# Two transformer blocks in split fp32 on one core: the passages between projections in two halves of 256 tokens

## The chip, the cores and the metric

The kernel runs on one core of one Trainium2 chip, as one launch. The metric is the time of one execution in device microseconds (us), as the median of several runs. The engines are PE (TensorE), ACT (ScalarE), DVE (VectorE), POOL (GpSimd) and SP (SyncE); weights arrive by DMA from HBM into SBUF, and matmuls write to PSUM, eight banks of 128 x 512 fp32 values.

## The reference, cut to what matters

512 tokens with 1024 features pass through two blocks. What matters here is the row of projections, and what stands between one and the next:

```python
def rms_norm(x, g):
    xf = x.astype(jnp.float32)
    y = xf * lax.rsqrt(jnp.mean(xf * xf, axis=-1, keepdims=True) + EPS)
    return (y * g.astype(jnp.float32)).astype(x.dtype)

# first_block: modulation, w_in, retention and sparse attention ("mixed"), then
        y = rmsnorm(mixed @ w_out[l], g_post[l])
        x = x + gate[:, None, :].astype(x.dtype) * y
# second_block
        f = swiglu(rms_norm(h, g_ffn1_pre[i]), w_ffn1_gate[i], w_ffn1_up[i], w_ffn1_down[i])
        h = h + 0.5 * rms_norm(f, g_ffn1_post[i])
        u = rms_norm(h, g_mix_pre[i])
        qkv = u @ w_in[i]
...
        h = h + rms_norm(mixed @ w_out[i], g_mix_post[i])
        f = swiglu(rms_norm(h, g_ffn2_pre[i]), w_ffn2_gate[i], w_ffn2_up[i], w_ffn2_down[i])
        h = h + 0.5 * rms_norm(f, g_ffn2_post[i])
        e = (p[i] @ w_ple_proj[i]) * jax.nn.sigmoid(h @ w_ple_gate[i])
        h = h + rms_norm(e, g_ple_post[i])
```

So each output is normed over its 1024 features, scaled, added to the residual, and the sum is normed again before the next projection. The hidden width of the FFNs is 2816, which is 22 tiles of 128.

## The kernel before

Tokens lie along the columns and features on the partitions, so the residual `X` and the input `UH`, `UL` of a projection are 8 tiles of 128 x 512 each. Every matmul of a projection is done in three parts on fp32r operands (`mm3`, L262 to L264): high times high, low times high, high times low. Weights come as a stream of 218 chunks of 512 KB into four slots `RAW`. For each chunk ScalarE makes the high part `WH` (`hi_of_weights`), VectorE subtracts it for the low part `WL` (`lo_of_weights`), two chunks ahead of TensorE, in two slots each.

The phases are, in order, with their chunks: p1 (32, input projection of block one), attention, p2 (8, output projection), f1 (44, gate and up of FFN1), d1 (24, down), p5 (24, input projection of block two), attention, p6 (8, output), f2 (44) and d2 (24) for FFN2, pp (2) and pg (8) for the last gated step. A chunk of p2, f1 and the like is `feature_chunk`: 8 feature tiles in three parts, 24 matmuls of 128x512, into one PSUM bank. In d1 and d2 three chunks make one output of 22 x 3 = 66 matmuls.

Each engine has its own program, written out by hand, and the engines wait for each other by counters: `mm` counts chunks that TensorE has finished, `w_hi` and `w_lo` split chunks, and an `Event` counts one kind of operation.

A *passage* is what stands between two projections. On ScalarE `project_out` and `mlp_down` take the square of each output tile and copy the tile (`Y_H`, `Y_U`); GpSimd adds up the squares (`sum_squares`, L435); TensorE sums over the partitions by two matmuls with ones (`summed_stats`, L1201 and L1203); ScalarE takes the root (`rms`) and VectorE the reciprocal (`rstd`, L814). Then for each of the 8 tiles VectorE forms gain times output times reciprocal (L1040), GpSimd adds it to `X` (L427), ScalarE writes the high part `UH` and the square, VectorE the low part `UL` (L1051 or L1049). The first chunk of the next projection waits tile by tile for `UL`, and the sums of the second norm are 8 matmuls with ones between its tiles (`first_of`, L1196). That norm's reciprocal is applied to the outputs of f1, not to its inputs. While the passage starts, TensorE does 34 matmuls whose result nobody reads (`bridge`, `keep_clock`, L1209):

```python
            def bridge(d):

                pe.wait_ge(w_lo, d + 1)
                keep_clock(34, WH[:, d % 2, 0:SEQ], B[7])
```

At the end the last passage adds to the residual on GpSimd (even tiles) and VectorE (odd tiles, L1029), and SyncE writes the output in 8 DMAs of 256 KB. `X` shares its place with other data during the first attention; GpSimd fetches it anew (L421) before the first passage.

Of the kernel before, what the change touches and what calls it, by code (L numbers as in the profile page):

```python
# [17 lines left out]
P = 128  # L18
SEQ = 512
DM = 1024  # L20
# [33 lines left out]
RAW_SLOTS = 4  # L54
SPLIT_SLOTS = 2
# [5 lines left out]
def build(nc, a):  # L61
    with ExitStack() as ctx:
# [7 lines left out]
        OFF_WL = OFF_WH + 8 * KB  # L70
        OFF_H = OFF_WL + 8 * KB
# [12 lines left out]
        RAW = at("RAW", OFF_RAW, [P, RAW_SLOTS, 1024])  # L84
        WH = at("WH", OFF_WH, [P, SPLIT_SLOTS, 1024], F32R)
        WL = at("WL", OFF_WL, [P, SPLIT_SLOTS, 1024], F32R)

# [45 lines left out]

        EP = hb("EP", 0, [P, KT, SEQ])
# [5 lines left out]
        AL = at("AL", OFF_WL, [P, 4, SEQ], F32R)  # L140
# [48 lines left out]
        raw_here = [sem(f"raw_here{n}") for n in range(RAW_SLOTS)]  # L189
# [19 lines left out]
        class Event:  # L209


            def __init__(self, name):
                self.sem, self.n = sem(name), 0
# [6 lines left out]
        def wait(eng, s, value):  # L220

            if value > 0:
                eng.wait_ge(s.sem if isinstance(s, Event) else s, value)
# [9 lines left out]
        def plan_banks():  # L233
# [10 lines left out]
            for first, up, down, s, n0 in (("p2", "f1", "d1", 1, 0), ("p6", "f2", "d2", 5, FT)):  # L244
# [3 lines left out]
                for m in range(8):  # L248
                    use(first, m, m % 4, E["y_copy"], 8 * ((s - 1) // 2) + m + 1)
# [3 lines left out]
                for m in range(8):  # L253
                    use(down, m, m % 4, E["y_copy"], 8 * ((s + 1) // 2) + m + 1)
            for m in range(8):
                use("pp", m, m % 4, E["ep"], m + 1)
            for m in range(8):
                use("pg", m, m % 4, E["pl_s"], m + 1)

        def mm3(out, lh, ll, rh, rl, start, stop, **kw):  # L260
# [7 lines left out]
            "silu_c converted ada_dot shift x_n gain_cols x_sq y_copy angle sines x_stats x_rms x_rstd u_t u_hi u_lo "  # L268
# [9 lines left out]
        x_odd = Event("x_odd")  # L278
        x_new, pl_y, at_x, at_m, at_hi, at_lo = (Event(n) for n in "x_new pl_y at_x at_m at_hi at_lo".split())
        f_g, f_s, f_u, f_h, f_hh, f_hl = (sem(n) for n in "f_g f_s f_u f_h f_hh f_hl".split())  # L280
        NSA = {n: Event("nsa_" + n) for n in "s max exp rec sc tr hi lo pv".split()}
        BAND = {n: Event("band_" + n) for n in "s max exp rec sc tr hi lo pv".split()}
        SBN = {n: Event("sbn_" + n) for n in "y sq st std rec m hi lo".split()}
        BDN = {n: Event("bdn_" + n) for n in "y sq st std rec m hi lo".split()}
# [15 lines left out]
        def square_tile(s, k):  # L300

            return SQ[:, k % 2, :] if s == 0 else T[8 + k % 2][:, :]


        SUMMED = (1, 3, 5, 7, 8)
        sq_sum = Event("sq_sum")
# [1381 lines left out]
```

## Time and profile before

| | us |
|---|---|
| median of 3 runs | 1782.75 |
| lowest and highest | 1782.35, 1784.17 |
| span of the profiled execution | 1785.6 |
| PE busy | 1655.7 |
| DVE busy | 864.7 |
| ACT busy | 662.8 |
| POOL busy | 236.9 |

The profiled execution is one more, and the profile gives its span as its time: 2.85 us above the median of the runs, 0.16%. Busy times are of that execution; an engine counts as busy while an instruction of its own runs. In a row of the trace, `UL<-X,VECS,UH` means that the instruction writes a tile of UL from tiles of the others. TensorE's weight loads are listed apart as PEld, and a matmul's own duration (some 0.39 us) is longer than its distance to the next one, since matmuls overlap; so the price of a matmul is read from starts, not from durations.

### The profile page before, as it was taken

The page shows a single profiled execution, that of the slowest core. Times are in us where ns is not written, and L with a number is a line of the kernel's source. Part 1 is how long each engine was busy: PE and PEld are TensorE (multiplying, and loading weights), DVE is VectorE, ACT ScalarE, POOL GpSimd, SP SyncE. Part 2 cuts the span into 40 slices and gives each one's busy share as a digit, 9 for nine tenths or more (in the row PEclk, how much of TensorE's full clock was granted, in tenths as well). Part 3 has the DMA queues.
Part 4 walks back from the last instruction along what each step waited for, and adds up shares of the span by engine and source line. Part 5 has one row for each costly group of instructions (what it writes and reads, how often), then busy time and mean ns, then how long its engine had stood idle before and what let it go on. Part 6 is the DMA issues. An engine that isn't in the chain of part 4 may idle for free.

```text
span 1785.6 us, 19927 instructions
## 1 busy us (share of the span) xinstructions
PE 1655.7 (93%) x7346; PEld 1270.9 (71%) x7346; DVE 864.7 (48%) x1264; ACT 662.8 (37%) x1135; POOL 236.9 (13%) x250
## 2 busy tenths in 40 slices
PE   2899999999898999999989999998989999999975
PEld 0678867665576888888867886655758888888753
DVE  7674636644426444442255436654364444422355
ACT  4333332344434333332233228844343333322332
POOL 4000000122223000000130002243230000001122
PEclk7999999899999999999999998989999999999987
DMA  9422330000131322233322321000113332233211
GB/s 378 151 92 88 107 116 8 0 1 1 60 106 37 103 96 94 94 95 107 106 69 72 99 90 48 1 1 24 61 40 101 96 103 95 94 118 106 94 47 48
DMA packets 39188, 144.95 MB, mean 81 GB/s; under 512 B 4288, under 2 KB 4304, under 8 KB 38608
## 3 DMA queue, kind: packets, MB, share of 16 engines
q1 hardware_dynamic: 37056, 131.65, 22.3%
q0 software_dynamic: 1488, 11.52, 1.7%
q8 instruction: 45, 0.74, 0.2%
q10 hardware_dynamic: 576, 0.85, 0.1%
q14 instruction: 23, 0.19, 0.0%
HBM read 141.91 MB, written 2.10 MB: 81 GB/s over the span
## 4 chain that ended last, share of the span: by engine, by line
PE 84%; DVE 11%; ACT 3%; issue 1%; DMA 1%; POOL 0%; SPq 0%; ACTq 0%; DVEq 0%
PE B L262 26%; PE B L264 23%; PE B L263 23%; PE B L1209 3%; DVE T L1040 2%; PE B L1389 2%; PE B L1521 1%; DVE T L814 1%; PE B L1381 1%; DVE WADA L839 1%; PE B L1196 1%; DVE UL L1051 1%; ACT T L474 1%; DVE NMAX L996 1%; DVE AL L1002 1%
## 5 line engine op out<-in xcount | busy, mean ns | idle before, releaser
L262 PE MATMUL B<-UH,WH 128*128 128x512 f32 x1120 | 448.8, 401 | 53.4 <-DVE UL L857 26.6
L263 PE MATMUL B<-UL,WH 128*128 128x512 f32 x1120 | 438.5, 392 | 0.0
L264 PE MATMUL B<-UH,WL 128*128 128x512 f32 x1120 | 438.4, 391 | 0.0
L474 ACT ACTIVATE WH<-RAW 128x1024 fp32r<-128x1024 f32 x218 | 230.7, 1059 | 471.6 <-PE B L264 471.5
L810 DVE TENSOR_TENSOR WL<-RAW,WH 128x1024 fp32r<-128x1024 f32 x130 | 160.1, 1233 | 368.2 <-ACT WH L474 368.1
L262 PEld LDWEIGHTS B<-UH,WH 128*128 128x128 f32 x1120 | 211.6, 189 | 120.7 <-issue 43.5
L263 PEld LDWEIGHTS B<-UL,WH 128*128 128x128 f32 x1120 | 211.9, 189 | 46.0 <-issue 3.8
L264 PEld LDWEIGHTS B<-UH,WL 128*128 128x128 f32 x1120 | 211.6, 189 | 44.6
L1062 DVE TENSOR_TENSOR WL<-RAW,WH 128x1024 fp32r<-128x1024 f32 x88 | 107.9, 1226 | 207.6 <-ACT WH L474 207.2
L262 PE MATMUL B<-HH,WH 128*128 128x512 f32 x352 | 136.9, 389 | 0.0
L263 PE MATMUL B<-HL,WH 128*128 128x512 f32 x352 | 136.9, 389 | 0.0
L264 PE MATMUL B<-HH,WL 128*128 128x512 f32 x352 | 136.9, 389 | 0.0
L435 POOL TENSOR_TENSOR T<-T,T 128x512 f32<-128x512 f32 x30 | 52.1, 1737 | 541.1 <-ACT T L474 541.1
L996 DVE TENSOR_REDUCE NMAX<-B 128x1 f32<-128x128 f32 (+1 forms) x96 | 46.7, 487 | 109.0 <-PE B L1382 108.8
L474 ACT ACTIVATE T<-T 128x512 f32<-128x512 f32 (+3 forms) x112 | 59.8, 537 | 89.0 <-DVE T L1065 85.7
L474 ACT ACTIVATE T<-B,NMAX 128x128 f32<-128x128 f32 (+1 forms) x96 | 50.6, 527 | 107.5 <-DVE NMAX L996 107.4
L474 ACT ACTIVATE T<-B 128x512 f32<-128x512 f32 (+2 forms) x117 | 63.2, 540 | 34.4 <-PE B L264 12.3
L264 PEld LDWEIGHTS B<-HH,WL 128*128 128x128 f32 x352 | 66.1, 188 | 13.8
L263 PEld LDWEIGHTS B<-HL,WH 128*128 128x128 f32 x352 | 66.1, 188 | 13.8
L262 PEld LDWEIGHTS B<-HH,WH 128*128 128x128 f32 x352 | 66.1, 188 | 13.6
L427 POOL TENSOR_TENSOR X<-X,T 128x512 f32<-128x512 f32 x36 | 60.9, 1701 | 91.7 <-DVE T L1040 91.7
L474 ACT ACTIVATE HH<-T 128x512 f32 x44 | 27.8, 632 | 119.6 <-DVE T L1070 119.6
(288 smaller groups left out, 2472.5 us busy)
## 6 DMA issues: line engine op xcount, KB each, us to landing
RAW<-in_stream SPq DMA_DIRECT2D x218, 512.0 KB, 3.4
WADA<-in_w_ada SPq DMA_DIRECT2D x6, 2048.0 KB, 20.6
W<-in_w POOLq DMA_DIRECT2D x2, 2048.0 KB, 11.7
X<-in_x SPq DMA_DIRECT2D x2, 1024.0 KB, 10.1
DECAY<-in_decay POOLq DMA_DIRECT2D x1, 2048.0 KB, 8.0
X<-in_x POOLq DMA_DIRECT2D x2, 1024.0 KB, 6.8
BIAS<-in_bias POOLq DMA_DIRECT2D x1, 2048.0 KB, 7.9
out<-X SPq DMA_DIRECT2D x8, 256.0 KB, 2.0
```

The lines of the kernel that those rows point to most:

```text
L262: nc.tensor.matmul(out, lh, rh, start=start, stop=False, **kw)
L263: nc.tensor.matmul(out, lh, rl, start=False, stop=False, **kw)
L264: return nc.tensor.matmul(out, ll, rh, start=False, stop=stop, **kw)
L427: x_new.mark(nc.gpsimd.tensor_tensor(X[:, k, :], X[:, k, :], T_RING[k % 4][:, :], ALU.add))
L435: sq_sum.mark(nc.gpsimd.tensor_tensor(T[7][:, :], square_tile(s, 0) if k == 1 else T[7][:, :], square_tile(s, k), ALU.add))
L474: return nc.scalar.activation(out, in_, func, **kw)
L810: tt(WL[:, d % 2, :], RAW[:, d % 4, :], WH[:, d % 2, :], ALU.subtract).then_inc(w_lo, 1)
L996: tag["max"].mark(v.tensor_reduce(NMAX[:, n % 8:n % 8 + 1], S_BANK[n % 3][:, 0:L], AX.X, ALU.max, negate=True))
L1040: E["u_t"].mark(stt(T_RING[n % 4][:, :], Y[:, n, :], gain[:, n:n + 1], T[7][:, :], ALU.mult, ALU.mult))
L1062: tt(WL[:, j % 2, :], RAW[:, nxt, :], WH[:, j % 2, :], ALU.subtract).then_inc(w_lo, 1)
L1209: mat(bank[:, :], operand[:, 0:P], operand, start=True, stop=True)
L1389: ins = nc.tensor.transpose(PT_BANK[u % 2][:, cols], S_RING[u % 4][:, cols], IDENT)
```

## The change

All passages are done in two halves of 256 tokens (`HALF`, `cols_of(t)`, with t counted through the kernel, even for the first half).

In p2, p6 and pg TensorE does eight half chunks (24 matmuls of 128x256) for the first half of the tokens, then eight for the second with the same weights, whose split parts are kept in eight places (`KEPT`) in memory that is free in that phase. In d1 and d2 there is no such place: the down weights are streamed and split twice, 48 chunks instead of 24 (`N_DENSE` 266 instead of 218), each with 24, 24 and 18 matmuls of 128x256. In f1, f2 and p5 the first four chunks are done for the first half, then for the second. All else of f1, f2, p5 and pp stays at 512 columns. The bridges are gone. The residual add moves from GpSimd to VectorE, the sums for the second norm from eight matmuls to GpSimd and two matmuls. `WL` is now written in the place of `RAW`, in four slots, so a load waits for TensorE's use of the chunk (`mm`) where it waited for the low part. VectorE waits for the second fetch of `X` ahead of the third low part of p2. The output is written in 16 DMAs of 128x256.

```diff
-D_P1, D_P2, D_F1, D_D1, D_P5, D_P6, D_F2, D_D2, D_PL = 0, 32, 40, 84, 108, 132, 140, 184, 208
-N_DENSE = 218
+D_P1, D_P2, D_F1, D_D1, D_P5, D_P6, D_F2, D_D2, D_PP, D_PG = 0, 32, 40, 84, 132, 156, 164, 208, 256, 258
+N_DENSE = 266
...
+        RAW = at("RAW", OFF_RAW, [P, SLOTS, 1024])
+        WH = at("WH", OFF_WH, [P, SLOTS, 1024], F32R)
+        WL = at("WL", OFF_RAW, [P, SLOTS, 1024], F32R)
...
+            def load(d, slot):
+                c = d - 24 * (d >= D_D1 + 24) - 24 * (d >= D_D2 + 24)
...
+            for d in range(SLOTS, N_DENSE):
+                if d - SLOTS in PHASE_OF:
+                    sp.wait_ge(w_lo, d - SLOTS + 1)
+                else:
+                    sp.wait_ge(mm, d - SLOTS + 1)
+                load(d, d % SLOTS)
```

ScalarE. `y_rms` and `n_rms` are the roots of the first and the second norm of a passage:

```diff
+            def y_rms(t):
+
+                wait(act, E["y_st"], 2 * t + 2)
+                E["y_rms"].mark(f(T[7][:, cols_of(t)], B[4][:, cols_of(t)], ACT.Sqrt, scale=1.0 / DM, bias=EPS))
+
+            def n_rms(t):
+
+                wait(act, E["n_st"], 2 * t + 2)
+                E["n_rms"].mark(f(T[6][:, cols_of(t)], B[5][:, cols_of(t)], ACT.Sqrt, scale=1.0 / DM, bias=EPS))
...
+            def project_out(phase, d0, t, scale, up):
...
+                    wait(act, E["half"], 8 * (t // 4) + m + 1)
+                    y_out(t, m, B[uses[phase, m][0]], Y_H)
+                y_rms(t)
+                for m in range(8):
                     act.wait_ge(mm, d0 + m + 1)
-                    bank = B[uses[phase, m][0]]
-                    squares(bank[:, :], s, m)
-                    E["y_copy"].mark(f(Y[:, m, :], bank[:, :], ACT.Copy))
-                rms(s, B[4], T[7])
...
+                    if m == 0:
+                        hi_of_weights(up)
+                        hi_of_weights(up + 1)
+                    elif m < 3:
+                        hi_of_weights(up + m + 1)
+                    y_out(t + 1, m, B[uses[phase, 8 + m][0]], Y_H)
+                    for k in ((), (), (0,), (1, 2), (3, 4), (5, 6), (7,), ())[m]:
+                        next_hi(t, k, scale)
+                n_rms(t)
+                y_rms(t + 1)
```

VectorE:

```diff
+            def y_rstd(t):
+
+                wait(dve, E["y_rms"], t + 1)
+                E["y_rstd"].mark(v.reciprocal(T[7][:, cols_of(t)], T[7][:, cols_of(t)]))
...
+            def next_u(t, n, Y, gain, scale, last_stage=False):
+
+                h = cols_of(t)
+                if n < KT:
+                    wait(dve, E["x_new"], 8 * t + n - 3)
+                    E["y_t"].mark(tt(T_RING[n % 4][:, h], Y[:, n, h], T[7][:, h], ALU.mult))
+                if 1 <= n <= KT:
+                    k = n - 1
+                    wait(dve, E["y_t"], 8 * t + k + 1)
+                    E["x_new"].mark(stt(X[:, k, h], T_RING[k % 4][:, h], gain[:, k:k + 1], X[:, k, h], ALU.mult, ALU.add))
+                if n >= 2 and not last_stage:
+                    k = n - 2
+                    wait(dve, E["nu_hi"], 8 * t + k + 1)
+                    if scale is None:
+                        E["nu_lo"].mark(tt(UL[:, k, h], X[:, k, h], UH[:, k, h], ALU.subtract))
+                    else:
+                        E["nu_lo"].mark(stt(UL[:, k, h], X[:, k, h], scale[:, k:k + 1], UH[:, k, h], ALU.mult, ALU.subtract))
 
 
...
+            def mlp_down(d0, t, gain, scale):
+
+                for c in range(48):
...
+                    if c == 25:
+                        y_rstd(t)
+                    if 26 <= c < 36:
+                        next_u(t, c - 26, Y_U, gain, scale)
+                    if c == 38 and scale is not None:
+                        n_rstd(t)
+
```

TensorE:

```diff
+            def n_stats(t):
+
+                h, c = cols_of(t), t
+                wait(pe, E["n_sum"], 6 * c + 6)
+                E["n_st"].mark(mat(B[5][:, h], ONES, T[4][:, h], start=True, stop=False))
+                wait(pe, E["n_sq"], 8 * c + KT)
+                E["n_st"].mark(mat(B[5][:, h], ONES, T[3][:, h], start=False, stop=True))
...
+            def half_chunk(d, out, uh, ul, t, done, ready=None, between=None):
+
+                h = cols_of(t)
+                hi, lo = kept_weights(*PHASE_OF[d]) if d in PHASE_OF else (WH[:, d % SLOTS, :], WL[:, d % SLOTS, :])
+                pe.wait_ge(w_lo, d + 1)
+                for k in range(KT):
+                    if ready is not None:
+                        ready(k)
+                    if between is not None and k == 5:
+                        between()
+                    ks = slice(k * P, (k + 1) * P)
+                    ins = mm3(out[:, h], hi[:, ks], lo[:, ks], uh(k)[:, h], ul(k)[:, h], k == 0, k == KT - 1)
+                if done is mm:
+                    ins.then_inc(mm, 1)
+                elif done is not None:
+                    done.mark(ins)
...
+            def mlp_up(phase, d0, n0, t):
                 for j in range(4):
-                    out = bank_of(phase, j)
-                    feature_chunk(d0 + j, out, *u_in, each=first_of(b, s) if j == 0 else None)
+                    between = None
+                    if j == 0:
+                        between = lambda: y_stats(t + 1)
+                    half_chunk(d0 + j, bank_of(phase, j), *u_in, t, None, between=between,
+                               ready=u_ready(t) if j == 0 else None)
+                n_stats(t)
+                for j in range(4):
+                    half_chunk(d0 + j, B[j], *u_in, t + 1, mm, ready=u_ready(t + 1) if j == 0 else None)
+                    if j == 1:
```

**Entry to f1 on TensorE, before.** Bank B3 takes the last output of p2; T7 and T9 hold sums and the last square, CONST the ones, and B0 is the first output of f1.

```order
L264 MATMUL B3<-UH_51,WL_57 128x512
L1201 MATMUL B4<-T7_123,CONST_138 128x512
L1203 MATMUL B4<-T9_125,CONST_138 128x512
L1209 MATMUL B7<-WH_56 128x512 x34
L262 MATMUL B0<-UH_51,WH_56 128x512
L263 MATMUL B0<-UL_52,WH_56 128x512
L264 MATMUL B0<-UH_51,WL_57 128x512
L262 MATMUL B0<-UH_51,WH_56 128x512
L263 MATMUL B0<-UL_52,WH_56 128x512
```

**The same place after the change,** a little further on: B3 is here the fourth output of f1 for the first half of the tokens, T4 and T3 hold the sums and the last square of the second norm.

```order
L268 MATMUL B3<-UH_51,WH_56 128x256
L269 MATMUL B3<-UL_52,WH_56 128x256
L270 MATMUL B3<-UH_51,WL_57 128x256
L1364 MATMUL B5<-T4_148,CONST_166 128x256 [waits n_sum]
L1366 MATMUL B5<-T3_147,CONST_166 128x256 [waits n_sq]
L268 MATMUL B0<-UH_51,WH_56 128x256 [waits nu_lo,w_lo]
L269 MATMUL B0<-UL_52,WH_56 128x256
L270 MATMUL B0<-UH_51,WL_57 128x256
L268 MATMUL B0<-UH_51,WH_56 128x256 [waits nu_lo]
```

The 34 matmuls of the bridge are gone, the first norm's two ones-matmuls have moved into the first half chunk of f1, and two ones-matmuls for the first half's second norm stand behind its fourth half chunk, ahead of the second half's first, which waits for `nu_lo`, the low parts of the second half.

**End of p2 on ScalarE, before.** The last output tile is squared and copied, then T7 is the root of the first norm.

```order
L474 ACTIVATE WH_56<-RAW_55 128x1024
L474 ACTIVATE T9_125<-B3 128x512
L474 ACTIVATE Y_H_74<-B3 128x512
L474 ACTIVATE T7_123<-B4 128x512
L474 ACTIVATE UH_51<-X_49,VECS_144 128x512
L474 ACTIVATE T8_124<-X_49 128x512
```

**The same place after the change.** T6 from B5 is the root of the first half's second norm, T7 from B4 that of the second half's first norm.

```order
L504 ACTIVATE UH_51<-X_49,VECS_172 128x256 [waits x_new]
L504 ACTIVATE T3_147<-X_49 128x256 [waits n_sum]
L504 ACTIVATE T9_153<-B3 128x256 [waits y_sum,mm]
L504 ACTIVATE Y_H_74<-B3 128x256
L504 ACTIVATE T6_150<-B5 128x256 [waits n_st]
L504 ACTIVATE T7_151<-B4 128x256 [waits y_st]
L504 ACTIVATE UH_51<-X_49,VECS_172 128x256 [waits x_new]
L504 ACTIVATE T2_146<-X_49 128x256
```

The root that starts the second half's passage (T7) now stands behind the root of the first half's second norm (T6), which waits for `n_st`, the two ones-matmuls of the place above.

**Down projection on ScalarE, before** (three weight splits, then one output):

```order
L474 ACTIVATE WH_56<-RAW_55 128x1024 x3
L474 ACTIVATE T8_124<-B0 128x512
L474 ACTIVATE Y_U_54<-B0 128x512
L474 ACTIVATE WH_56<-RAW_55 128x1024 x3
```

**After, in its second half:**

```order
L504 ACTIVATE WH_56<-RAW_55 128x1024
L504 ACTIVATE UH_51<-X_49,VECS_172 128x256
L504 ACTIVATE T2_146<-X_49 128x256
L504 ACTIVATE WH_56<-RAW_55 128x1024
L504 ACTIVATE UH_51<-X_49,VECS_172 128x256
L504 ACTIVATE T3_147<-X_49 128x256
L504 ACTIVATE WH_56<-RAW_55 128x1024
L504 ACTIVATE T9_153<-B1 128x256
```

**and on VectorE, the same stretch:**

```order
L903 TENSOR_TENSOR WL_57<-RAW_55,WH_56 128x1024
L927 TENSOR_TENSOR T11_155<-Y_U_54,T7_151 128x256
L931 SCALAR_TENSOR_TENSOR X_49<-T10_154,SC_175,X_49 128x256
L903 TENSOR_TENSOR WL_57<-RAW_55,WH_56 128x1024
L927 TENSOR_TENSOR T0_144<-Y_U_54,T7_151 128x256
L931 SCALAR_TENSOR_TENSOR X_49<-T11_155,SC_175,X_49 128x256
L938 SCALAR_TENSOR_TENSOR UL_52<-X_49,VECS_172,UH_51 128x256
```

Between two weight splits there now stand the high part and the square of a tile of the next input (UH, T2) on ScalarE, and its product, residual add and low part on VectorE, each waiting for the other engine.

## Rows read from the trace of the kernel before

**Rows 1.** The page: busy time, share of the span and instructions of each engine.

```profile
PE 1655.7 (93%) x7346; PEld 1270.9 (71%) x7346; DVE 864.7 (48%) x1264; ACT 662.8 (37%) x1135; POOL 236.9 (13%) x250
```

**Rows 2.** Windows: us; busy PE, PEld, DVE, ACT, POOL; granted clock, DMA share, GB/s.

```profile
529.11:558.89 29.78, 23.78 (x79) 13.80 (x78) 22.53 (x18) 12.69 (x20) 13.77 (x8) 1.00 0.06 19
559.00:798.00 239.00, 238.86 (x1054) 197.27 (x1053) 113.44 (x132) 76.00 (x90) 0.00 (x0) 1.00 0.29 95
798.00:913.35 115.35, 115.35 (x511) 95.51 (x510) 29.06 (x25) 32.75 (x39) 11.04 (x6) 1.00 0.33 105
913.35:944.47 31.12, 24.54 (x80) 14.78 (x78) 22.91 (x18) 12.69 (x20) 12.79 (x8) 0.95 0.10 32
1301.11:1330.88 29.77, 23.79 (x80) 13.83 (x78) 22.52 (x18) 12.70 (x20) 13.74 (x8) 1.00 0.06 19
...
1685.31:1722.74 37.43, 24.37 (x77) 16.16 (x76) 23.52 (x20) 13.35 (x22) 14.00 (x8) 0.82 0.17 55
...
1761.04:1785.60 24.56, 3.65 (x4) 1.18 (x4) 15.96 (x14) 3.63 (x5) 7.89 (x5) 0.62 0.23 85
```

**Rows 3.** Chain of waits in the passage from p2 to f1: start us, us, what.

```profile
532.82 3.37 DVE T L814
...
537.04 1.74 POOL X L427
...
541.01 1.69 DVE T L1040
...
560.13 3.37 DVE T L814
```

**Rows 4.** Groups by line and form: count, busy us, mean ns, idle before and releaser.

```profile
L810 DVE TENSOR_TENSOR WL<-RAW,WH 128x1024 fp32r<-128x1024 f32 x130 | 160.1, 1233 | 368.2 <-ACT WH L474 368.1
L1134 DVE TENSOR_TENSOR AL<-T,AH 128x256 fp32r<-128x256 f32 x8 | 3.3, 416 | 0.4 <-ACT AH L474 0.4
L474 ACT ACTIVATE WH<-RAW 128x1024 fp32r<-128x1024 f32 x218 | 230.7, 1059 | 471.6 <-PE B L264 471.5
L474 ACT ACTIVATE AH<-T 128x256 fp32r<-128x256 f32 x16 | 6.6, 413 | 17.9 <-PE B L264 9.4 <-DVE T L938 8.5
L435 POOL TENSOR_TENSOR T<-T,T 128x512 f32<-128x512 f32 x30 | 52.1, 1737 | 541.1 <-ACT T L474 541.1
L263 PEld LDWEIGHTS B<-UL,WH 128*128 128x128 f32 x1120 | 211.9, 189 | 46.0 <-issue 3.8
```

**Rows 5.** Timeline of TensorE behind an idle stretch in pg: start us, us, engine, line.

```profile
1707.51 0.77 PE L262 MATMUL B<-UH,WH 128*128 128x512 f32 x1 [6.24 <-DVE WL L810]
1708.08 0.63 PE L263 MATMUL B<-UL,WH 128*128 128x512 f32 x1
1708.51 0.63 PE L264 MATMUL B<-UH,WL 128*128 128x512 f32 x1
```

**Rows 6.** DMA issues: count, KB each, median us from issue to landing.

```profile
RAW<-in_stream SPq DMA_DIRECT2D x218, 512.0 KB, 3.4
X<-in_x POOLq DMA_DIRECT2D x2, 1024.0 KB, 6.8
out<-X SPq DMA_DIRECT2D x8, 256.0 KB, 2.0
```

**Rows 7.** Timeline where p2 starts: the second fetch of X, and TensorE.

```profile
484.59 1.57 POOL L387 DMA_DIRECT2D X<-in_x  x2 [11.90 <-DVE T L1018]
...
485.45 0.50 PE L262 MATMUL B<-MRH,WH 128*128 128x512 f32 x1 [1.11 <-DVE UL L1022]
```

**Rows 8.** Timeline of TensorE: 47 matmuls of 128x280 in p1, and a 64x256 pair.

```profile
203.43 0.29 PE L263 MATMUL B<-WL,UH 128*128 128x280 f32 x1
...
209.34 0.29 PE L264 MATMUL B<-WH,UL 128*128 128x280 f32 x1
...
357.73 0.28 PE L263 MATMUL B<-KNL,QNH 64*128 64x256 f32 x1
357.85 0.28 PE L264 MATMUL B<-KNH,QNL 64*128 64x256 f32 x1
```

More of the change, by code:

```diff
@@ L243, in plan_banks @@
                 n += P1_KIND[d] != TOK
-            for first, up, down, s, n0 in (("p2", "f1", "d1", 1, 0), ("p6", "f2", "d2", 5, FT)):
+            for first, up, down, t, n0 in (("p2", "f1", "d1", 0, 0), ("p6", "f2", "d2", 4, FT)):
                 if first == "p6":
@@ new lines, in sum_n, with sums @@
+            def sum_n(t, k):
+                h, c = cols_of(t), t
+                wait(pool, E["n_sq"], 8 * c + k + 1)
+                if k >= 2:
+                    wait(pool, E["n_sum"], 6 * c + k - 1)
+                E["n_sum"].mark(nc.gpsimd.tensor_tensor(T[4][:, h], T[2][:, h] if k == 1 else T[4][:, h],
+                                                        T[2 + k % 2][:, h], ALU.add))
+            def sums(t, order):
+                for who, k in order:
+                    if who == "y":
+                        sum_y(t + 1, k)
+                    else:
+                        sum_n(t, k)
@@ L443, in _ @@
+            sums(2, LONG)
+            for k in range(1, 7):
+                sum_n(3, k)
             pool.wait_ge(mm, D_P6)
@@ L501, in rms, with squares @@
+            def squares(src, k):
+                wait(act, E["x_stats"], k - 1)
+                return E["x_sq"].mark(f(SQ[:, k % 2, :], src, ACT.Square))
+            def rms(bank, tile):
+                wait(act, E["x_stats"], KT)
                 E["x_rms"].mark(f(tile[:, :], bank[:, :], ACT.Sqrt, scale=1.0 / DM, bias=EPS))
@@ L1056, in mlp_up, with project_out @@
-            def mlp_up(d0, n0):
-                with dve.Fori(0, 11) as i:
+            def project_out(d0, t, gain, scale, up):
+                for m in range(2, 8):
+                    lo_of_weights(d0 + m)
+                y_rstd(t)
+                for n in range(KT + 2):
+                    next_u(t, n, Y_H, gain, scale)
+                    if n < 8 and n % 2 == 0:
+                        lo_of_weights(up + n // 2)
+                n_rstd(t)
+                y_rstd(t + 1)
+                for n in range(KT + 2):
+                    next_u(t + 1, n, Y_H, gain, scale)
+                n_rstd(t + 1)
+                wait(dve, E["n_rstd"], t + 2)
@@ L1255, in _ @@
             for k in range(KT):
-                stats(0, k, B[5])
+                stats(k, B[5])
             for d in range(32):
```

524 lines of the change are left out of this document (292 added, 232 removed).

## The prediction

> **What bounds the kernel now.** I read the page first: the engines' busy shares say that TensorE works for 93% of the span [rows 1], so only two things can move the time: the 7% in which it does no work of use, and the price of its matmuls. The windows say where that 7% is [rows 2]. Inside a projection TensorE never stops: 1054 matmuls fill 239 us, 0.2268 us each, and the first down projection, from 798 to its end, is 115.35 us busy of 115.35. Around each passage it is different. From the last matmul of the output projection to the second chunk of FFN1 29.8 us go by, of which one chunk of 24 matmuls, 5.44 us, is work; the 34 keep-clock matmuls and idle time are the rest. The same holds before FFN2 (29.8), after the first down projection (31.1), and in smaller measure after the second (37.4, with 72 matmuls, 16.3 us, of work). The tail is 24.6 us with no work at all. Exposed, by window minus work: 24.3 + 24.3 + 25.7 + 21.1 + 24.6 = 120.0 us.
>
> The chain of waits says what fills a passage [rows 3]: a reciprocal on VectorE, 3.37 us, then per feature tile a product on VectorE (1.69) that takes turns with GpSimd's residual add (1.74), then a second reciprocal, 3.37. All of it is proportional to the tokens and waits for the whole projection before it.
>
> **What the change does to the passages, part by part.** A half passage has 256 columns. VectorE takes 0.42 us for such an operation and ScalarE 0.41; splitting one weight chunk takes 1.06 (ScalarE) and 1.23 (VectorE) at any width [rows 4]. A reciprocal of 256 columns I take as half of 3.37, 1.7. The add leaves GpSimd for VectorE, so a tile is three VectorE operations, 1.25 us, plus the turns that GpSimd's sums of squares still take (one is 1.3 to 1.7 us at 512 columns [rows 4], half that here): 1.4 to 1.6 us a tile, an estimate. A half chunk of TensorE is 24 x 0.1183 = 2.84 us (the 0.1183 is worked out below).
>
> *First half, output projections.* Its passage, 0.4 + 1.7 + 8 x 1.6 = 15 us, runs beside the second half's eight half chunks, 22.7 us. Hidden.
>
> *Second half, output projection to FFN (twice).* Cover is four half chunks of FFN on the first half, 11.4 us. But ScalarE's order puts the root of the first half's second norm ahead of the root of the second half's first norm, and the former waits for two matmuls that TensorE issues only behind those four half chunks. So the second half's chain, which could start at once, starts 12.4 us after the projection ends: root, two reciprocals in a row (2 x 1.7), first tile: 18.7. TensorE idles for 6.2 us there. A stop of 6.24 us has a row: after it the same 128x512 matmuls come 0.43 us apart instead of 0.2268, the 1.2 GHz level [rows 5]; a row of them costs some 2.2 us, as it did there. With seven more tiles of 1.4 us, the last chunk of five ends at about 29.0, so 14.8 not worked; plus 2.2 for the clock, 1.0 for the small ones-matmuls, and 2.0 for the third to fourth weight chunk, whose split is queued on VectorE behind the whole second half. In all 20.0, where 24.3 stood: saves 4.3, twice.
>
> *Down projection 1.* Its first half's passage is laid over chunks 25 to 38 of 48. A half down chunk lasts (2 x 2.84 + 2.13)/3 = 2.6 us. ScalarE and VectorE now hand each other work inside one chunk: split high 1.06, split low 1.23, product 0.42, add 0.42, next high part 0.41, square 0.41: 3.9 us in a ring, for eight chunks, against 2.6. That is 10.4 in all; the two chunks that are split ahead absorb one lead, 2.6: 7.8 us of stalls. The second down projection has no squares, a ring of 3.5, so 7.2 less 2.6: 4.6, taken as 4.5.
>
> *Down 1 to projection p5.* The second half's passage (about 15 us) stands beside four half chunks, 11.4: 2.8 idle, 0.7 at the start, 2.1 slow clock, 2.0 for stats matmuls: 7.6 for 25.7. *Down 2 to the last gate.* The 48 matmuls of the small projection (10.9 us, full width) and eight half chunks follow: 6.8 for 21.1, mostly waits for banks and one function table. *Tail.* The same steps at 256 columns and only for the second half: last square and its sum 1.5 (the first half's leftover tiles lie beside it), ones-matmuls and root 1.2, reciprocal 1.7, nine steps of two VectorE operations, 0.84 by their durations and 0.7 each by my estimate of their overlap, 6.3, issue and landing 2.2 [rows 6]: 12.9 for 24.6.
>
> *An added wait.* VectorE now waits for the second fetch of x before it splits the third weight chunk of the output projection. The fetch, two of 1 MB, lands 6.8 us after issue (median; 512 KB of weights 3.4 [rows 6]), the second being issued at about 485.4, while TensorE starts at 485.45 [rows 7] and wants that chunk after two half chunks, at 491.1. With the last landing at about 493.2 and 1.23 for the split it is 494.5: 3.4 us of stall. Queued behind it are all later splits, but those then run ahead.
>
> *Removed at nothing:* the keep-clock bridges (their time is inside the windows above), GpSimd's adds (moved, counted). *Added at nothing:* 8 more output DMAs, since all but the last lie beside the tail; the kept weights, since the second half needs no split at all.
>
> Sum after: 20.0 x 2 + 7.6 + 6.8 + 12.9 + 3.4 + 7.8 + 4.5 = 83.0. Saved: **37.0 us**.
>
> **What the halves cost TensorE.** 1920 matmuls of 512 columns become 3840 of 256 (output projections and gate 1152, first four chunks of the two FFNs and p5 576, down 2112). No row has 128x256 in this form. The nearest has 128x280: 46 steps from 203.43 to 209.34, 0.1285 each [rows 8]. A line through 280 at 0.1285 and 512 at 0.2268 gives 0.1183 at 256. From below: exactly half, 0.1134, at no cost. From above: the 0.12 between two neighbours of 64x256 [rows 8], or no less than 0.1285 itself. I take 0.1183, on the line between measured points: 3840 x 0.1183 - 1920 x 0.2268 = **+18.8** (bounds 0 and +58; 6.5 more at 0.12). The weight load is 189 ns [rows 4], longer than that step, and yet the 280-column rows follow at 0.1285, so loads run two deep beside matmuls there. The Trainium skill (TensorE: Matmul & The Clock Gate, What overlaps and what doesn't) says that a weight load overlaps with matmuls in flight only when its row group differs; by that each of the 1920 further loads of 0.189 would be paid in full, +363 in the place of +18.8. The trace's 0.1285 per 280-column matmul, less than one load, disagrees with it.
>
> **Twice-streamed down weights.** 48 chunks instead of 24 per FFN at twice the rate. A slot is free when its chunk is used, three chunks before it is needed again: 3.4 landing + 1.06 + 1.23 + 0.2 = 5.9 against 3 x 2.6 = 7.8. Slack 1.9, so nothing; the DMA engines were 33% busy there [rows 2], about 66% now.
>
> **Sum.** -37.0 + 18.8 = -18.2 on the profiled execution's 1785.6, i.e. 1767.4; that execution stands 2.9 above the runs' median of 1782.75, so 1764.6: **1765 us**.
>
> **The rivals.** A measurement of this kernel can tell about 0.2%, 3.6 us.
> (a) *Starved by the stream, slower.* TensorE would wait for w_lo in both down stages. If with two or three loads under way the landing grows from 3.4 to L, a chunk takes (L + 2.5)/3. The slack is gone at L = 5.3, the whole gain at 5.9; at the 6.8 that 1 MB took, 96 chunks x 0.5 = +48, 1813. For it: doubled rate beside 33% DMA share. Against: 512 KB land at 3.4 with another under way. Chance 0.05.
> (b) *256 columns held at the 280's 0.1285, slower.* +39 on the sum, 1804; decides from 0.1231 per matmul. For it: the load of 189 ns, if two can just be hidden in 0.25 us. Against: the 64x256 pair at 0.12. Chance 0.05.
> (c) *The clock does not hold on half matmuls, slower.* If they came at the low level's 0.43/2 = 0.215, 3840 of them would cost +370, 2135. Against: the 280-column stretch ran at 0.1285, where the low level would give 0.43 x 280/512 = 0.235. The Trainium skill (same page, Why this matters for your kernels) counts thin matmuls among the things that let the clock swing, and asks for loops over the contraction without a break, which these are. Chance 0.02.
> (d) *The work laid beside the matmuls hurts more than priced* (rings in both downs twice as long, GpSimd's sums excluding VectorE): +10 to +20, 1775 to 1785. Chance 0.14, of it 0.08 still faster by more than 0.2% and 0.06 within.
> (e) *Clock holds and stalls overlap:* without the 2.2s, the 2.0s and half the ring stalls, -15: 1750. Chance 0.18.
>
> **How the numbers follow.** Forecast (1756 to 1775) 0.56, (e) 0.18, (d) 0.14, (a) to (c) 0.12. Range 1748 to 1780: it takes in (e) nearly whole, most of (d), and 0.12 at matmul price; left out are (a) to (c) and the ends. Faster than 1779.2: 0.56 + 0.18 + 0.08 = 0.82. Same 0.06. Slower 0.12.
>
> **What would show it.** Neighbouring 128x256 matmuls 0.118 apart; windows at the two FFN entries with some 6 us of TensorE idle behind the fourth half chunk, released by VectorE's low parts; ring stalls of 1.2 us per chunk in chunks 27 to 35 of down; RAW landing under 4.5 us there; tail near 13. A spacing above 0.123 or TensorE waiting on weight splits throughout down would make the prediction wrong.

## The result and the profile after

| | before | changed |
|---|---|---|
| median of 20 runs, us | 1788.58 | 1794.88 |
| lowest, highest | 1782.35, 1801.84 | 1788.72, 1800.57 |
| span of the profiled execution | 1785.6 | 1793.8 |

The ratio of changed to before is 1.0035, 95% interval 1.0021 to 1.0049: the change makes the kernel **slower by about a third of a per cent**. The forecast was 1765 us and faster by 1%, with a range up to 1780; direction and range were both missed. On spans the change is +8.2 us where -18.2 was forecast. The comparison below goes by spans, because the three runs on which the forecast stood (1782.75) lay low: over 20 runs the kernel before has a median 5.8 us higher, so that part of the distance from 1765 to 1794.88 is not the change's.

The page of the changed kernel, the lines that answer to [rows 1, 4, 6]:

```profile
PE 1652.6 (92%) x9160; PEld 1369.0 (76%) x9160; DVE 952.4 (53%) x1476; ACT 721.6 (40%) x1329; POOL 217.6 (12%) x280
L504 ACT ACTIVATE WH<-RAW 128x1024 fp32r<-128x1024 f32 x242 | 253.3, 1050 | 119.4 <-DMA RAW<-in_stream 108.7
RAW<-in_stream SPq DMA_DIRECT2D x266, 512.0 KB, 3.6
X<-in_x POOLq DMA_DIRECT2D x2, 1024.0 KB, 7.4
```

Nothing here tells a slower kernel from a faster one: TensorE is as busy as before and no engine is full. A page of totals must be cut at the places where the work is the same in both. I took six stages, from the first matmul of p2 on; each ends where the first matmul of the next phase starts. Windows of the kernel before (columns as in [rows 2]):

```profile
485.45:793.67 308.22, 302.07 (x1303) 243.73 (x1304) 142.03 (x154) 102.03 (x130) 25.44 (x15) 1.00 0.29 94
793.67:913.35 119.68, 119.68 (x530) 99.10 (x529) 31.57 (x28) 34.17 (x40) 11.04 (x6) 1.00 0.32 102
913.35:1253.09 339.74, 317.75 (x1409) 228.28 (x1408) 175.99 (x318) 167.93 (x359) 72.32 (x105) 0.95 0.14 47
1253.09:1565.62 312.53, 305.46 (x1302) 245.01 (x1303) 150.83 (x163) 105.32 (x134) 24.78 (x14) 0.99 0.26 86
1565.62:1687.72 122.10, 121.27 (x533) 99.61 (x532) 33.78 (x30) 37.15 (x44) 12.01 (x7) 1.00 0.34 108
1687.72:1785.60 97.88, 64.70 (x246) 48.18 (x244) 54.53 (x47) 29.33 (x44) 28.47 (x18) 0.83 0.14 49
```

and of the changed kernel, the same stages and then the entry to f1:

```profile
486.28:803.18 316.90, 299.54 (x1553) 259.04 (x1553) 154.37 (x189) 102.56 (x165) 22.13 (x25) 0.96 0.28 88
803.18:941.01 137.83, 131.62 (x1065) 130.04 (x1064) 73.52 (x78) 67.45 (x98) 19.39 (x18) 0.99 0.59 182
941.01:1262.70 321.69, 299.95 (x1460) 223.41 (x1459) 167.08 (x326) 160.62 (x358) 64.88 (x103) 0.96 0.16 52
1262.70:1581.43 318.73, 302.01 (x1552) 260.82 (x1553) 163.35 (x198) 105.79 (x169) 21.44 (x24) 0.96 0.26 81
1581.43:1714.87 133.44, 129.29 (x1061) 127.87 (x1060) 72.79 (x77) 64.44 (x90) 17.76 (x13) 1.00 0.60 192
1714.87:1793.80 78.93, 62.33 (x446) 58.46 (x444) 44.76 (x84) 34.26 (x66) 9.07 (x12) 0.92 0.23 78
539.97:585.45 45.48, 32.53 (x206) 29.75 (x205) 24.34 (x39) 13.70 (x31) 6.83 (x9) 0.81 0.13 38
```

The granted clock shows where something differs: it was 1.00 and 0.99 from p2 to d1 and from p6 to d2, and is 0.96 in both now. The spacing of half matmuls is read from the timeline of the changed kernel, in an unbroken stretch of d1; 472 matmuls start from the first row to the last, 0.1202 us apart:

```profile
809.30 0.38 PE L268 MATMUL B<-HH,WH 128*128 128x256 f32 x1 [0.21 <-DVE WL L903]
...
865.91 0.28 PE L268 MATMUL B<-HH,WH 128*128 128x256 f32 x1
```

Half width costs 3840 x 0.1202 - 435.5 = +26.1 us, in each stage by its share. What is left of each difference is what the passages gained or lost:

| stage | difference | of it half width | the rest | forecast of the rest |
|---|---|---|---|---|
| before p2 | +0.8 | 0 | +0.8 | 0 |
| p2 to d1 | +8.7 | 3.9 | +4.8 | -0.9 |
| d1 | +18.2 | 7.2 | +11.0 | +7.8 |
| d1 to p6 | -18.1 | 1.3 | -19.4 | -18.1 |
| p6 to d2 | +6.2 | 3.9 | +2.3 | -4.3 |
| d2 | +11.3 | 7.2 | +4.1 | +4.5 |
| pp to end | -19.0 | 2.6 | -21.6 | -26.0 |
| sum | +8.2 | 26.1 | -17.9 | -37.0 |

Between d2 and the last row 2.4 us have to be moved: from d2's last matmul to pp's first 2.64 us went by before and 0.12 now, and the forecast counts that to the passage behind d2. So moved, d2 lost 6.5 us where 4.5 was forecast, and the last row gained 24.0 where 26.0 was.

The passage out of d1 and the end behave as forecast or nearly. Where the first half's passage lies beside p2 and p6, the stages should have gained and lost instead. The timeline at the entry to f1 in the changed kernel, TensorE's starts:

```profile
554.73 0.59 PE L1366 MATMUL B<-T,CONST 128*128 128x256 f32 x2
561.61 0.55 PE L268 MATMUL B<-UH,WH 128*128 128x256 f32 x1 [6.28 <-DVE UL L938]
```

and the chain of waits there:

```profile
554.46 0.43 PE B L1364 x2
554.90 0.45 PE B L1366 x2
555.36 0.39 ACT T L504
555.78 0.31 DVE T L920
556.09 1.36 issue
557.45 1.71 DVE T L913
559.18 0.76 DVE T L927 x2
559.94 0.40 DVE X L931
```

The two ones-matmuls of the first half's second norm (L1364, L1366) release both roots, then both reciprocals follow, then the first product: the queue of the forecast, to the tenth of a microsecond (6.3 us of idle time for 6.2). So the mechanism was seen, and yet the stage came out 5.7 us worse than its sum.

Two more places show in the timeline of the changed kernel. At the start of p6 TensorE waits for VectorE's low parts, where the same wait was 0.10 us before; and in d1 half matmuls come 0.21 us apart from 907.5 to 910.9, behind two stops of 1.84 us and four of 0.4 to 0.7:

```profile
1268.22 0.39 PE L268 MATMUL B<-MBH,KEPT_W 128*128 128x256 f32 x1 [2.62 <-DVE MBL L1291]
...
906.93 0.36 PE L268 MATMUL B<-HH,WH 128*128 128x256 f32 x1 [1.84 <-DVE WL L903]
...
908.10 0.41 PE L269 MATMUL B<-HL,WH 128*128 128x256 f32 x1
908.32 0.41 PE L270 MATMUL B<-HH,WL 128*128 128x256 f32 x1
```

The experiments take the parts one at a time.

### The profile page after: what moved, and what is told of

Read it like the earlier page. It is cut to its first block, busy times and chain, and to the rows that moved or that the text cites. A ratio compares the mean times of both kernels' runs of the same rounds, so it can differ in the third digit from the quotient of the medians.

```text
span 1793.8 us, 23305 instructions
## 1 busy us (share of the span) xinstructions
PE 1652.6 (92%) x9160; PEld 1369.0 (76%) x9160; DVE 952.4 (53%) x1476; ACT 721.6 (40%) x1329; POOL 217.6 (12%) x280
## 4 chain that ended last, share of the span: by engine, by line
PE 78%; DVE 12%; ACT 4%; issue 2%; DMA 2%; POOL 1%; SPq 0%; DVEq 0%; ACTq 0%; POOLq 0%
PE B L268 24%; PE B L269 22%; PE B L270 22%; PE B L1372 2%; DVE WL L903 2%; PE B L1573 2%; DVE X L931 1%; ACT WH L504 1%; PE B L1565 1%; DMA X<-in_x 1%; DVE T L927 1%; DVE WADA L962 1%; PE B L1709 1%; DVE NMAX L1119 1%; DVE UL L938 1%
## 5 line engine op out<-in xcount | busy, mean ns | idle before, releaser
L268 PE MATMUL B<-UH,WH 128*128 128x512 f32 (+1 forms) x1120 | 429.2, 383 | 54.2 <-DVE UL L980 26.3
L269 PE MATMUL B<-UL,WH 128*128 128x512 f32 (+1 forms) x1120 | 420.6, 376 | 0.0
L270 PE MATMUL B<-UH,WL 128*128 128x512 f32 (+1 forms) x1120 | 420.2, 375 | 0.0
L268 PE MATMUL B<-HH,WH 128*128 128x256 f32 x704 | 201.8, 287 | 10.4 <-DVE WL L903 10.4
L269 PE MATMUL B<-HL,WH 128*128 128x256 f32 x704 | 199.9, 284 | 0.0
L270 PE MATMUL B<-HH,WL 128*128 128x256 f32 x704 | 199.8, 284 | 0.0
L268 PEld LDWEIGHTS B<-HH,WH 128*128 128x128 f32 x704 | 135.7, 193 | 13.2 <-issue 6.5
L269 PEld LDWEIGHTS B<-HL,WH 128*128 128x128 f32 x704 | 135.7, 193 | 0.2
L270 PEld LDWEIGHTS B<-HH,WL 128*128 128x128 f32 x704 | 135.8, 193 | 0.0
L504 ACT ACTIVATE T<-B 128x256 f32<-128x256 f32 (+4 forms) x165 | 71.3, 433 | 146.4 <-PE B L270 89.9
```

What stands on the lines that cost most here:

```text
L268: nc.tensor.matmul(out, lh, rh, start=start, stop=False, **kw)
L269: nc.tensor.matmul(out, lh, rl, start=False, stop=False, **kw)
L270: return nc.tensor.matmul(out, ll, rh, start=False, stop=stop, **kw)
L504: return nc.scalar.activation(out, in_, func, **kw)
```

## The experiments

**The wait for X.** VectorE's wait moved from ahead of p2's splits to behind them:

```diff
-            dve.wait_ge(x_again, 32)
             project_out(D_P2, 0, GC, VECS[:, V_F1PRE:V_F1PRE + 8], D_F1)
...
                     lo_of_weights(d0 + m)
+                if t == 0:
+                    dve.wait_ge(x_again, 32)
                 y_rstd(t)
```

> The changed kernel with VectorE's wait for the second fetch of X moved behind the six weight splits of p2. My theory: the stop of 4.6 us at the third weight chunk of p2 and the 2.0 us of slow clock behind it go, so 6 to 7 us less than the changed kernel and nothing else moves. Rival: TensorE is only let go to meet another late part (the split queue, or X itself at the first product); then 0 to 3 us less.

Median 1787.28; ratio to before 0.9996 (0.9968 to 1.0024), 0.4% under the changed kernel's. Span 1785.5, and the stage from p2 to d1 fell from 316.90 to 310.10, 6.8 us. The rival, another late part behind the first, is out. In the changed kernel the stop and what follows it are

```profile
492.02 0.28 PE L270 MATMUL B<-UH,KEPT_L 128*128 128x256 f32 x1
496.71 0.55 PE L268 MATMUL B<-MRH,KEPT_H 128*128 128x256 f32 x1 [4.41 <-DVE KEPT_L L901]
497.06 0.42 PE L269 MATMUL B<-MRL,KEPT_H 128*128 128x256 f32 x1
497.28 0.41 PE L270 MATMUL B<-MRH,KEPT_L 128*128 128x256 f32 x1
```

4.6 us without a start, then half matmuls 0.21 apart until 501.2, some 2 us more. The forecast had 3.4 for the stop and nothing for the clock behind it, which these rows show at its lower level, 1.2 GHz.

**The order of the roots.** The second half's root and reciprocal go ahead of the first half's second norm, at both FFN entries:

```diff
# ScalarE
-                n_rms(t)
                 y_rms(t + 1)
...
                     next_hi(t, k, scale)
+                n_rms(t - 1)
                 n_rms(t)
# VectorE
-                n_rstd(t)
                 y_rstd(t + 1)
                 for n in range(KT + 2):
                     next_u(t + 1, n, Y_H, gain, scale)
+                n_rstd(t)
                 n_rstd(t + 1)
# TensorE
                     if j == 1:
+                        wait(pe, E["n_rms"], t + 1)
                         n_stats(t + 1)
```

> The changed kernel with the second half's root and reciprocal ahead of the first half's second norm, on ScalarE and VectorE, at both FFN entries. My theory (the queued root sets the idle 6.3 us): the second half's low parts begin some 10 us earlier, the idle stretch and its slow clock go, and some stall per tile stays at 1.6 us a tile; 7 to 9 us less at each entry, 14 to 18 in all. Rival (GpSimd's late sums and VectorE's pace set it, not the order): the first low part comes only 3 us earlier, 5 to 7 us less in all.

Median 1766.61; ratio 0.9870 (0.9824 to 0.9916), 1.6% under the changed kernel's. Windows from p2 to d1 and from p6 to d2:

```profile
483.34:785.35 302.01, 292.97 (x1552) 254.14 (x1553) 154.47 (x189) 102.56 (x165) 22.17 (x25) 0.99 0.29 92
1246.20:1549.85 303.65, 295.85 (x1553) 256.27 (x1553) 163.45 (x198) 105.81 (x169) 21.46 (x24) 0.98 0.27 85
```

14.9 and 15.1 us less than in the changed kernel, twice what I had written down, so my size was a miss though its direction held. From the first half chunk of f1 to its first full chunk 45.48 us became 30.97, of which 23.1 are matmuls. The root that starts the second half's chain comes 4.8 us after the entry starts, where it came 15.4 after it. First its row in the changed kernel (both roots in one row), then in this one:

```profile
555.36 0.66 ACT L504 ACTIVATE T<-B 128x256 f32<-128x256 f32 x2 [11.66 <-PE B L1366]
```

```profile
541.48 0.38 ACT L504 ACTIVATE T<-B 128x256 f32<-128x256 f32 x1 [1.10 <-PE B L1358]
```

The chain is that much earlier, and since all tiles hang on it, the idle time (6.3), most of the waits between tiles (0.3 to 0.6 us each, of which two are left, 0.31 and 0.65) and the slow clock go together. Of the 7.9 us that are still not worked at this entry, 1.73 are TensorE's wait for GpSimd's last sum and 1.72 its wait for a weight split that VectorE has queued behind the second half's tiles; no experiment touched the latter, and it is still there in the fastest kernel.

**One tile per two down chunks.** The passage of the first half is laid over chunks 26 to 47 of the down projection instead of 25 to 38, with GpSimd's order of sums adapted:

```diff
# ScalarE
-                    if 27 <= c < 35:
-                        next_hi(t, c - 27, scale)
+                    if 27 < c < 44 and c % 2 == 0:
+                        next_hi(t, (c - 28) // 2, scale)
# VectorE
-                    if 26 <= c < 36:
-                        next_u(t, c - 26, Y_U, gain, scale)
+                    if 25 < c < 45 and c % 2 == 0:
+                        next_u(t, (c - 26) // 2, Y_U, gain, scale)
```

> The changed kernel with one tile of the next input at every second chunk of the down projections instead of at every chunk. My theory (a ring of ScalarE and VectorE longer than one half chunk makes the stalls): the 7.3 us of stalls in d1 and the 4.7 in d2 fall to under 2 and 1, 9 to 12 us less. Rival (the doubled weight stream lands late): the waits for split weights stay about as long, 0 to 3 us less.

Median 1783.99; ratio 0.9995 (0.9963 to 1.0026), so the time alone doesn't show it: the ten runs lie between 1778.53 and 1798.13, and the profiled one, span 1776.8, is the fastest of them. The stages do show it. The stretch of half matmuls in d1 fell from 137.7 to 129.9 us, that of d2 from 133.3 to 128.7: 12.4 together, as expected. What TensorE and the loads did in d1, first in the changed kernel, then in this one (who waited for `WL`: us, times; then the loads):

```profile
  PE B L268: 6.2, 7
RAW<-in_stream SPq DMA_DIRECT2D x48, 512.0 KB, 4.1
```

```profile
  PE B L268: 0.4, 2
RAW<-in_stream SPq DMA_DIRECT2D x48, 512.0 KB, 4.2
```

The ring was the cause, and the stream was not: 512 KB landed in 4.1 and 4.2 us (median), where it was 3.4 in the kernel before at half the rate, and the waits went all the same.

**Half width alone.** The kernel before, with 80 full chunks of FFN1 and FFN2 as two halves each and no passage touched:

```diff
-                        for k in range(KT):
-                            ins = mm3(B[j][:, :], wtile(WH, j, k), wtile(WL, j, k), UH[:, k, :], UL[:, k, :], k == 0, k == KT - 1)
+                        for h in (slice(0, 256), slice(256, 512)):
+                            for k in range(KT):
+                                ins = mm3(B[j][:, h], wtile(WH, j, k), wtile(WL, j, k), UH[:, k, h], UL[:, k, h], k == 0, k == KT - 1)
```

> The kernel before with the 80 later chunks of FFN1's and FFN2's gate and up done as 24 matmuls on one half of the columns and 24 on the other, same weights: 3840 half matmuls for 1920, as many as in the change. My theory: 0.1203 us each as in the change's trace, so 26 us more than the kernel before, 1.5%. Rival (the line I forecast with, 0.1183): 19 us more; a third, that only the streamed stage paid for it: under 10 us more.

Median 1818.08; ratio to before 1.0155 (1.0108 to 1.0201). Span 1811.8, 26.2 us above 1785.6; the two stages that were edited, p2 to d1 and p6 to d2, have 12.8 each of it. So the price is the width's own, 0.1200 per matmul (834 starts from 600.03 to 699.99), and it is paid with the weights streamed once too.

**All three edits.**

> The three edits together: late wait for X, second half's root first, one tile per two down chunks. My theory: they lie in different stages and add up: the first took the changed kernel's span from 1793.8 to 1785.5, the second to 1762.2, the third to 1776.8; stage by stage that is 6.5 + 30 + 12, so a span of about 1745, 2.3% below the kernel before. Rival: part of what the single edits showed is drift outside the edited stages (p1 and attention moved by up to 3 us); then 1750 to 1755.

Median 1746.37; ratio **0.9784** (0.9758 to 0.9811) to the kernel before: 2.2% faster, and by the two ratios 2.5% under the changed kernel's. Span 1744.2. They add up: by stages the three took 6.8, 30.0 and 12.4 us one at a time, 49.2 together, and the span fell by 49.6. Windows: p2 to d1, d1, p6 to d2, d2:

```profile
485.25:780.97 295.72, 291.33 (x1552) 252.73 (x1553) 154.63 (x189) 102.57 (x165) 22.18 (x25) 1.00 0.29 94
780.97:910.73 129.76, 129.19 (x1065) 128.30 (x1064) 72.49 (x77) 67.38 (x98) 21.66 (x18) 1.00 0.61 192
1231.13:1535.33 304.20, 296.04 (x1552) 256.60 (x1553) 163.42 (x198) 105.81 (x169) 21.47 (x24) 0.98 0.27 85
1535.33:1664.00 128.67, 128.25 (x1062) 127.64 (x1061) 72.64 (x77) 64.12 (x90) 18.65 (x13) 1.00 0.63 199
```

The clock is 1.00 from p2 to the end of d1, where TensorE's longest stops are now 1.74 us (for GpSimd's sum) and 1.72 (for the split).

**The ones-matmuls one half chunk later.** In addition, `between = lambda: y_stats(t + 1)` for `j == 1` instead of `j == 0`, to spare TensorE a stop of 1.7 us for GpSimd's last sum.

> As the one before, and the second half's ones-matmuls moved from the first half chunk of the FFN to its second one. My theory: TensorE's stop of 1.7 us for GpSimd's sums goes at both entries, but the chain behind the ones-matmuls, which now ends the stage, starts 1 us later: 0 to 2 us less than the three. Rival: the late start costs as much as the stop: no change.

Neither the gain nor the rival's "no change": it got slower. Median 1757.95; ratio 0.9859 (0.9811 to 0.9907), and span 1757.1, 12.9 above the three edits. The entry to f1 took 35.50 us instead of 30.96. The root came 7.2 us after the entry's start instead of 4.8; so 2.4 us at the head of the chain cost 4.5 at its end. Windows of that entry, first with four edits (from 0.9 us ahead of it), then with three:

```profile
533.00:569.40 36.40, 30.81 (x214) 28.98 (x212) 25.33 (x40) 13.70 (x31) 7.72 (x9) 0.91 0.16 48
```

```profile
532.30:563.24 30.94, 26.55 (x206) 25.44 (x205) 24.42 (x39) 13.69 (x31) 6.87 (x9) 1.00 0.19 58
```

The clock fell to 0.91 where it had been 1.00: it is at its lower level from 553.2 to 560.0, and what stood before were waits between tiles of 0.69, 0.98 and 0.98 us, none longer, where the three edits have 0.30 and 0.64. A short stop early is cheaper here than a late chain. The entry to f2 cost 3.8 us more in the same way (p6 to d2 307.97 for 304.20). Another 4.6 us of the span lie between d1 and p6, where nothing was edited; that stretch moved by up to 5 us among the kernels with halves in down.

**Matmuls in the idle time.** The changed kernel, with a bridge as the kernel before had one:

```diff
                 n_stats(t)
+                keep_clock(26, WH[:, d0 % SLOTS, 0:SEQ], B[7])
                 for j in range(4):
```

> The changed kernel with 26 matmuls of 128x512 that nobody reads in the idle 6.3 us at both FFN entries, nothing else. My theory: they fit in the idle time and keep the clock at its high level, which is worth the 24 matmuls that came 0.1 us late, 2 to 3 us an entry, 4 to 6 in all. Rival: VectorE's pace of 1.6 us a tile sets the stage and the slow clock costs nothing: within 1 us.

The rival was right, on one run. Span 1790.3, but the entry to f1 took 45.45 us (45.48 without), p6 to d2 318.68 (318.73). The clock there was 0.89 instead of 0.81 and it bought nothing. TensorE went on to wait for the low parts:

```profile
558.64 0.28 PE L269 MATMUL B<-UL,WH 128*128 128x256 f32 x1
558.75 0.28 PE L270 MATMUL B<-UH,WL 128*128 128x256 f32 x1
559.95 0.39 PE L268 MATMUL B<-UH,WH 128*128 128x256 f32 x1 [0.92 <-DVE UL L938]
```

Three half matmuls per tile fit between two tiles 1.6 us apart at either level, so while the tiles come, the clock costs nothing. And with waits of 0.6 to 1.0 us between tiles it was low again by 563: behind the last tile 23 half matmuls from 568.06 on still came 0.21 apart, as 24 do in the changed kernel from 571.22 on. So the some 2 us that the clock costs at an entry weren't had by filling the idle stretch alone; with three edits, where the tiles are on time, they are had without it.

**The halves in down undone.** With the four edits, and again with the three, the down projections as they were before the change (24 chunks of 128x512, one stream; `pair_out` squares and copies both halves of an output, and both passages follow):

```diff
-                for c in range(48):
+                for c in range(24):
                     hi_of_weights(d0 + c + 2)
...
-                        y_out(t + c // 24, c // 3 % 8, B[uses[phase, c // 3][0]], Y_U)
...
+                        pair_out(t, c // 3, B[uses[phase, c // 3][0]], Y_U)
```

> The four edits but with the down projections as they were before the change: 24 chunks, 128x512, each weight streamed once; their passages follow after them, still half by half. It undoes one part of the change. My theory: the halves in down buy about what they cost; against the kernel with four edits d1 and d2 are 10 and 9 us shorter, the way from d1 to p5 some 13 and from d2 to the gate some 6 longer: within 4 us of it. Rival (the halves in down are what the change lives on): 10 us or more slower.

> The kernel with three edits (span 1744.2) but with whole down projections, each weight streamed once, so that only the output projections, the FFN entries and the gate are in halves. It repeats the comparison of the halves in down on the kernel without the late ones-matmuls. My theory: span 1744 to 1749, the halves in down being worth 0 to 4 us; rival (they carry a good part of the gain once the ring is loosened): 1752 or more.

Against the kernel with four edits: median 1756.67, span 1755.4 (1757.1 with halves). With three: median 1750.99, ratio to before 0.9775 (0.9719 to 0.9831), span 1749.7 (1744.2 with halves), just above the 1744 to 1749 that I had expected. The medians of the two pairs differ by -1.3 and +4.6 us, the ratios' intervals overlap in both. So 24 more DMAs of 512 KB and 528 more matmuls per down projection buy at most a few microseconds: with them d1 is 10 us longer and the way from d1 to p6 13 to 20 us shorter, d2 is 9 us longer and the way from its last matmul to the end 6 us shorter.

**The start of p6.** With three edits, at p6 the tiles k < 4 of two half chunks stand ahead of their tiles k >= 4 (a loop over `part` in 2, `m` in 2 and `k` in `range(4 * part, 4 * part + 4)`).

> The kernel with three edits, and at the start of p6 the four feature tiles of k < 4 of the first two half chunks before their tiles of k >= 4, which wait for VectorE. My theory: in the change half as much work stands in front of that wait as before, which cost 3 to 4 us of the stage p6 to d2 (where the passage alone does not explain the difference between FFN1 and FFN2); it comes back: 304.2 becomes 301 to 302. Rival: the clock is low there anyway and the wait only moves: no change.

The stage p6 to d2 fell from 304.20 to 302.00, 2.2 us, at the near edge of the 301 to 302 that I had expected. It can't be seen in the time: median 1746.56, span 1744.1, since the unedited stretch before p6 was 3.1 us longer in this trace. The part is shown in its stage, its worth as a whole is open.

**Everything together,** with GpSimd's last two sums swapped.

> The kernel with three edits, the p6 start, and GpSimd's last sum of the second half's output squares ahead of its last sum of the first half's next squares. My theory: 3 us from the p6 start, and TensorE's stop of 1.7 us in the first half chunk of each FFN shrinks by one sum of 0.8 us, twice: a span of 1739 to 1740. Rival: that sum waits for ScalarE's square, which comes as late: the stop stays.

Median 1743.79; ratio **0.9746** (0.9696 to 0.9797), the fastest kernel of the study; from the three edits it can't be told apart. Span 1743.2, where I expected 1739 to 1740. TensorE's stop in the first half chunk of f2 shrank from 1.74 to 1.20, by less than a sum of 0.8: the sum that now comes first had to wait for ScalarE's square (1.88 us of idle time before it at the entry to f1), which is in part the rival.

## Why the prediction was wrong

No single cost explains it: the mechanisms were mostly right and their sizes were not. The sum missed the spans by 26.4 us: 7.3 for the half matmuls, 12.3 in the two stages with an FFN entry (p2 to d1 5.7, p6 to d2 6.6), 3.2 in d1, 2.0 in d2, 2.0 behind d2 and 0.8 ahead of p2; the way from d1 to p6 came out 1.3 better. The step that failed is thus the sum for the stages with an FFN entry, and next to it the price of a half matmul. Its steps, in order:

- *What bounds the kernel, and how much stands open (120 us).* Right. The passages out of d1 and at the end gained 19.4 and 24.0 us, for 18.1 and 26.0.
- *Half matmuls at 0.1183.* Too low, and this is the largest single term: 0.1200 to 0.1202, so +26.1 for +18.8. I had taken the line through 280 and 512 columns; the lone pair of neighbours at 256 in [rows 8], 0.12, was the better reading, and I used it only as a bound. The rival at 0.1285 did not come.
- *"In all 20.0, where 24.3 stood: saves 4.3, twice."* This is the step that failed: with the 3.4 for X the stage p2 to d1 was to gain 0.9 and lost 4.8, and p6 to d2 was to gain 4.3 and lost 2.3. At either entry 22.4 us were not worked (at f1 45.48 - 23.1), so 2.4 more than the sum had: the tiles come 1.6 us apart, not 1.4, and TensorE's stop of 1.7 us for GpSimd's sum inside the first half chunk was left out. (The forecast also put one of GpSimd's sums at 1.3 to 1.7 us at 512 columns; the mean in [rows 4] is 1.74.) Inside p6 itself 4.9 us were lost that had no term at all: 0.7 for the ones-matmuls, and the rest at its start, where half a chunk covers VectorE's late operands half as long (2.62 us of waiting where it was 0.10; the experiment on p6 got 2.2 us back, the other 2 stay open). The 0.7 for the ones-matmuls was left out in p2 too; 0.7 us of short holds that the kernel before had behind each entry went away and made up for it.
- *The queued root.* It was seen, and priced as one delay of 6.2 us beside late tiles and a slow clock; it was not asked what the passage would do without it. The second experiment answers: 15 us at each entry. With that order put right the stages gain 16.9 (p2 to d1, without the stop for X) and 12.8 us (p6 to d2), width apart; the change as it was written gave 15 away in each by the order of two instructions.
- *3.4 us for the wait for X.* 6.8: the later of the two fetches landed 9.0 us after issue, where the forecast had 7.8 from the kernel before (493.2 less 485.4), so the stop was 4.6, and 2 us of slow clock follow it, as they follow the other one. I priced the clock at one idle stretch and forgot it at the other.
- *7.8 and 4.5 us for the ring in down.* 11.0 and 6.5 with the ones-matmuls. In d1 7.3 of them are gaps that TensorE spent waiting for weight splits, and 1.4 are 15 half matmuls at the lower clock behind these gaps, which the forecast left out. The third experiment took away 7.8 and 4.6.
- *Twice-streamed weights: nothing.* Right. Landing 4.1 us against the 5.3 where the slack ends. The rival stays out.
- *Sum.* -37.0 + 18.8 became -17.9 + 26.1. The forecast was a difference of two large terms, and the width, both FFN entries, the wait for X, both downs and the end all missed to the same side. The range ended at 1780 as if such misses would cancel. Rival (d), stalls that hurt more than priced, has the right direction with too small a size, but not by the causes it named: the downs lost 11.0 and 6.5 us and not twice 7.8 and 4.5, and that GpSimd's sums exclude VectorE was not shown.

## What to carry to other kernels

When work is cut in halves to hide one behind the other, read on each in-order engine what stands ahead of the *second* half's first instruction: one root queued behind a sum that TensorE delivers late was worth 30 us here over two entries, more than the 17.9 us that all the passages had gained on balance. Price the halves' own cost at once (here 26 us for 3840 matmuls) and add to each stop of several microseconds the slow clock behind it (2 us at each of three stops here). And a scheme that pays in one stage and not in another can be kept in part: half-width down projections were worth little here, the halves at the output projections and FFN entries nearly all.

## What was not expected of the hardware

- A 128x256 matmul costs 0.1200 to 0.1202 us in a chain, 6% over half of the 0.2268 of 128x512, though its weight load shows 0.19 us; 128x280 costs 0.1285.
- Of GpSimd's 96 sums of 128x256 in the changed kernel 69 took 0.7 to 0.9 us each, and most others 1.4 to 1.72, in places where VectorE is at work on the tiles: the sum that TensorE waits for at the entry to f1 stands behind one such. That VectorE's work is the cause was not tried.
- The granted clock was low behind stops of 4.4 us and 6.3 us (half matmuls 0.21 apart), and stayed at 1.00 with three edits over a stage with single stops of 1.74 and 1.72 us. The longest stop alone doesn't tell: it was low for 3.4 us in d1 of the changed kernel behind stops of 1.84 us with shorter ones around them, and for 6.8 us at the entry with four edits behind waits of 0.69 and 0.98 us between tiles.
